# Every expert pair behind the branches to the further rounds, three branches for seven trips, and an earlier start for four weight chunks

## The chip, the cores and the metric

The kernel runs on one core of a Trainium2 chip. The metric is the device time of one execution in microseconds, the median over several. The engines are TensorE (PE in the rows), VectorE (DVE), ScalarE (ACT), GpSimd (POOL) and SyncE (SP), which issues nearly all DMAs.

## What is computed

One decoder block on 512 tokens of width 1024. The first half mixes tokens: a norm, a wide input projection, retention and an mLSTM, gates, an output projection and a residual add. Nothing of its arithmetic changes. The second half is a mixture of 32 experts, of which each token uses two:

```python
group_prob = softmax(xf @ w_group + b_group); g_w, g_idx = top_k(group_prob, 1)
top_logits, e_idx = top_k(sel_logits, TOP_K)          # 2 of the 8 experts of that group
weights = g_w * softmax(top_logits)
def expert_block(args):                               # 1024 -> 512 -> 1024 per expert
    xb, e = args
    return (silu(xb @ w_gate[e]) * (xb @ w_up[e])) @ w_down[e]
out = segment_sum(ys * slot_w[:, None], slot_tok, ...)  # residual add and final norm follow
```

All 32 experts are passed whatever the routing says, so 192 MB-sized pieces of weights are always read.

## The kernel before

Each engine has a program written by hand; the order on it is the order of the code, and engines wait for each other by semaphores. Of the mixture:

- **Pairs.** Two experts are worked on at once, each with up to 64 tokens (`CAP`): 16 pairs, one `pair` each. A pair's weights are 12 chunks of 1 MiB (`moe_chunk`): four of gate, four of up, four of down. They go through a ring of 18 slots, `raw_moe`, of 8 KB per partition. A slot's chunk is loaded when TensorE has used what was in it (`wait_chunk_used`), and no more than four chunks are in flight (`IN_FLIGHT`).
- **TensorE in a pair.** `gate_or_up` four times (half a gate or up product, 16 matmul rows in the trace, two chunks used), `turn_x` (transposes the next pair's gathered tokens), `turn_h`, `down` twice, and `combine` of the pair before (adds its result to the tokens). `last_pair` is the 16th pair.
- **The tables.** The router's result becomes two tables: which token sits in which slot (`tok_tab`; the product in line 723 makes it, and GpSimd gathers rows of x by it into `xg`), and which weight (`slot_tab`; product of line 733).
- **Rounds.** An expert with more than 64 tokens needs more rounds. Each engine reads the largest count with `value_load` and passes a loop of seven trips (`Fori(1, ROUNDS, 1)`), with an `If(most > r * CAP)` over the code of a whole round in it. With these inputs no round runs, and every trip jumps over the body. In front of this loop stand 15 pairs, behind it the 16th: the loop stands at line 774 on TensorE and at line 411 on SyncE, where the last 12 chunks are issued behind it.
- **The opening.** Into the ring go first 8 chunks, as the places of older tiles come free (lines 391 to 397), then `x2` is stored to `x_scratch` for the gather (line 400), then 8 chunks more, and the last two after the router's logits (`lg_ps`), since their slots lie on `h2T`.

Of the kernel before, what the change touches and what calls it, by code (L numbers as in the profile page):

```python
# [68 lines left out]
LAST_CHUNKS = R_CHUNKS - PAIR_CHUNKS  # L69
SP_LOOPS = (LAST_CHUNKS - MOE_RAW) // (2 * MOE_RAW)  # L70
# [23 lines left out]
def hybrid_block(nc, x, norm_mix_w, w_in, ret_gn_w, w_ret, conv_w, conv_b, b_i, b_f, mlstm_gn_w, w_mlstm, w_out,  # L94
                 norm_ffn_w, w_group, b_group, w_router, b_router, w_gate, w_up, w_down, norm_final_w, consts, out):
    ctx = ExitStack()
    with ctx:
# [6 lines left out]
        def sem(name):  # L104
# [27 lines left out]
                   enumerate([64, 72, 0, 8, 16, 24, 80, 88, 32, 40, 48, 56, 96, 104, 112, 120, 144.5, 152.5])]  # L132
# [9 lines left out]
        h2T = at("h2T", 144.5, [P, KD, T])  # L142
# [12 lines left out]
        squares = at("squares", 168.5, [P, TT, D])  # L155
# [19 lines left out]
        def small(name, shape, dt=F32):  # L175
# [64 lines left out]
        at_ok = sem("slots_ready")  # L240
# [21 lines left out]
            "one_hot_ready", "table_in_psum", "table_ready", "counts_ready"))  # L262
# [17 lines left out]
        def wait_chunk_used(eng, r, i, m):  # L280

            n, kind, half, a = chunk_of(m)
            if half == 0:
                eng.wait_ge(first_used, r * (6 * PAIRS) + i * (6 * LOOP_PAIRS) + 6 * n + 2 * kind + 2)
            else:
                eng.wait_ge((g_f, u_f, y_f[1])[kind], r * (2 * PAIRS) + i * (2 * LOOP_PAIRS) + 2 * n + 2)

# [15 lines left out]
        def _(sp):  # L303
# [72 lines left out]
            def round_chunks(r):  # L376
                if not isinstance(r, int):
                    for m in range(LAST_CHUNKS, R_CHUNKS):
                        moe_chunk(m, r - 1, 0, True)
                    for m in range(MOE_RAW):  # L380
                        moe_chunk(m, r, 0, True)
# [3 lines left out]
                for m in range(MOE_RAW + SP_LOOPS * 2 * MOE_RAW, LAST_CHUNKS):  # L385
                    moe_chunk(m, r, 0, True)
# [28 lines left out]
            for m in range(LAST_CHUNKS, R_CHUNKS):  # L415
                moe_chunk(m, extra, 0, True)
# [9 lines left out]
        def _(pe):  # L426
# [211 lines left out]
            def gate_or_up(r, i, n, up, half):  # L638
# [4 lines left out]
                if half == 0 and (not isinstance(N, int) or N > 0):  # L643
# [19 lines left out]
            def down(r, i, n, half):  # L663

                N, m = r * PAIRS + i * LOOP_PAIRS + n, PAIR_CHUNKS * n + 8 + 2 * half
                if half == 0:
                    pe.wait_ge(hf_ok, N + 1)
                    if not isinstance(N, int) or N > 0:
# [45 lines left out]
            def moe_round(r):  # L714
                N0 = r * PAIRS
                if not isinstance(r, int):
                    last_pair(r - 1)
                    combine(N0 - 1, range(8))
# [8 lines left out]

                pe.wait_ge(at_ok, r + 1)
                pe.wait_ge(ww_ok, 1)
                for n in range(2 * TT):  # L730
# [6 lines left out]
                turn_x(N0, 0)  # L737
                turn_x(N0, 1)
                for half in range(2):
                    gate_or_up(r, 0, 0, 0, half)  # L740
                for half in range(2):
                    gate_or_up(r, 0, 0, 1, half)
                turn_x(N0 + 1, 0)
                turn_h(N0)
                down(r, 0, 0, 0)
                turn_x(N0 + 1, 1)
                down(r, 0, 0, 1)
# [45 lines left out]
        def _(act):  # L793
# [191 lines left out]
            def square(t):  # L985
                act.wait_ge(free[t], BLOCKS)
                nc.scalar.activation(squares[:, t, :], x2[:, t, :], ACT.Square, accum_out=ssq[:, t:t + 1]).then_inc(sq_ok, 1)
# [19 lines left out]
            act.wait_ge(e2_ok, 1)  # L1007
            nc.scalar.activation(stat[:, 1, 0:TT], rt[:, 6, 0:TT], ACT.Sigmoid)
# [16 lines left out]
            def moe_round(r):  # L1025
                N0 = r * PAIRS
                if not isinstance(r, int):
                    pair(N0 - 1, last=True)
                pair(N0, first=isinstance(r, int))
                with act.Fori(0, PAIRS - 2, 1) as i:  # L1030
                    pair(N0 + i + 1)

            moe_round(0)
            act.wait_ge(cnt_ok, 1)
            most = act.value_load(cnt[0:1, 0:1], min_val=0, max_val=T)
            with act.Fori(1, ROUNDS, 1) as r:
                with act.If(most > r * CAP):
                    moe_round(r)


            extra = act.value_load(cnt[0:1, 1:2], min_val=0, max_val=ROUNDS - 1)
            pair(extra * PAIRS + (PAIRS - 1), last=True)
# [13 lines left out]
        def _(dve):  # L1056
# [354 lines left out]
            def pair(N, first=False, last=False, bare=False):  # L1411
# [16 lines left out]
                if first:  # L1428
                    dve.wait_ge(ir_in, 16)
# [6 lines left out]
            def moe_round(r):  # L1436
                N0 = r * PAIRS
                if not isinstance(r, int):

                    pair(N0 - 1, last=True)  # L1440
                    add(N0 - 1, range(8))
# [8 lines left out]
                V.tensor_tensor(at_slot[:, :, :, :].rearrange("p k t s -> p (k t) s"), where, slots, ALU.is_equal).then_inc(at_ok, 1)  # L1450
                if isinstance(r, int):
                    own(V.reduce_max(rt[:, 7, 40:41], cb[:, 1, TT * NE:(TT + 1) * NE], AX.X))
                dve.wait_ge(tab_ps, r * 2 + 2)
                V.tensor_scalar(tok_tab[:, :], cb[:, 2, 0:PAIRS], float(NO_TOKEN), None, ALU.add).then_inc(tab_ok, 1)
                if isinstance(r, int):
                    weights()
# [187 lines left out]
```

## Time and profile before

| | us |
|---|---|
| median of 3 runs (lowest, highest) | 1087.26 (1085.89, 1087.49) |
| the profiled execution, its own time | 1088.14 |
| span of its trace | 1086.4 |
| TensorE busy | 1013.1 |
| the mixture's pairs, from the first gate matmul to the last pair's down | 599 to 1069 |

The time of the profiled execution is 1.7 us over its span, and 0.9 us over the median. "Issue" in a chain is time in which an engine waited for nothing that the profile shows. A q behind an engine's name means its sequencer: PEldq is that of TensorE.

### The profile page before, as it was taken

The page shows a single profiled execution, that of the slowest core. Times are in us where ns is not written, and L with a number is a line of the kernel's source. Part 1 is how long each engine was busy: PE and PEld are TensorE (multiplying, and loading weights), DVE is VectorE, ACT ScalarE, POOL GpSimd, SP SyncE. Part 2 cuts the span into 40 slices and gives each one's busy share as a digit, 9 for nine tenths or more (in the row PEclk, how much of TensorE's full clock was granted, in tenths as well). Part 3 has the DMA queues.
Part 4 walks back from the last instruction along what each step waited for, and adds up shares of the span by engine and source line. Part 5 has one row for each costly group of instructions (what it writes and reads, how often), then busy time and mean ns, then how long its engine had stood idle before and what let it go on. Part 6 is the DMA issues. An engine that isn't in the chain of part 4 may idle for free.

```text
span 1086.4 us, 12967 instructions
## 1 busy us (share of the span) xinstructions
PE 1013.1 (93%) x4661; PEld 649.7 (60%) x4661; DVE 425.0 (39%) x733; ACT 276.6 (25%) x462; POOL 70.4 (6%) x102
## 2 busy tenths in 40 slices
PE   4999999999999999999993999999999999889874
PEld 4888888888888888888883333333333333333322
DVE  4236356434533334535524123333333232333316
ACT  5343564433333336413221000000000000000002
POOL 0564000000000000000000000000000000000000
PEclk9999999999999999999995999999999999999978
DMA  7313222222222222245829799999999999999791
GB/s 273 116 55 141 78 78 78 78 78 78 78 78 78 93 101 79 77 127 171 328 109 395 303 421 420 420 421 421 421 421 420 420 417 421 421 420 418 303 383 78
DMA packets 59959, 263.83 MB, mean 243 GB/s; under 512 B 9152, under 2 KB 9216, under 8 KB 35208
## 3 DMA queue, kind: packets, MB, share of 16 engines
q1 hardware_dynamic: 57432, 257.94, 60.2%
q0 software_dynamic: 2480, 5.26, 1.3%
q8 instruction: 30, 0.49, 0.2%
q14 instruction: 17, 0.14, 0.0%
HBM read 263.17 MB, written 4.20 MB: 246 GB/s over the span
## 4 chain that ended last, share of the span: by engine, by line
PE 55%; DMA 39%; issue 2%; DVE 2%; SPq 1%; ACT 0%; DVEq 0%; POOLq 0%; ACTq 0%
PE pj L463 45%; DMA raw_moe<-in_w_gate_dram 13%; DMA raw_moe<-in_w_up_dram 13%; DMA raw_moe<-in_w_down_dram 12%; PE pj L650 2%; PE cb L429 2%; DMA xg<-x_scratch,tok_tab 1%; PE cb L608 1%; PE cb L482 1%; PE pj L676 1%; PE cb L508 1%; DMA vrow<-in_mlstm_conv_w_dram 1%; PE cb L550 1%; PE cb L512 0%; PE cb L515 0%
## 5 line engine op out<-in xcount | busy, mean ns | idle before, releaser
L650 PE MATMUL pj<-raw_moe,xT 128*64 128x512 f32 x1024 | 233.0, 604 | 25.2 <-issue 10.2
L1070 DVE TENSOR_TENSOR wl<-raw_mix,wh 128x1024 fp32r<-128x1024 f32 x88 | 109.1, 1245 | 183.3 <-ACT wh L807 183.0
L650 PEld LDWEIGHTS pj<-raw_moe,xT 128*64 128x64 f32 x1024 | 75.1, 139 | 168.0 <-issue 168.0
L463 PE MATMUL pj<-wh,hTh 128*128 128x512 f32 x320 | 130.1, 407 | 1.6 <-DVE hTl L1098 1.6
L463 PE MATMUL pj<-wl,hTh 128*128 128x512 f32 x320 | 125.3, 392 | 0.0
L463 PE MATMUL pj<-wh,hTl 128*128 128x512 f32 x320 | 125.0, 391 | 0.0
L807 ACT ACTIVATE wh<-raw_mix 128x1024 fp32r<-128x1024 f32 x88 | 92.4, 1057 | 121.9 <-PE pj L463 111.1
L1403 DVE TENSOR_TENSOR x<-x,cb 128x512 f32<-128x512 f32 x120 | 77.0, 683 | 103.7 <-PE cb L687 103.7
L676 PE MATMUL pj<-raw_moe,hf 128*64 128x512 f32 x512 | 116.7, 598 | 0.8 <-ACT hf L1018 0.8
L463 PE MATMUL pj<-hTh,wh 128*128 128x512 f32 x192 | 80.2, 418 | 0.0
L463 PE MATMUL pj<-hTh,wl 128*128 128x512 f32 x192 | 75.4, 393 | 0.0
L463 PE MATMUL pj<-hTl,wh 128*128 128x512 f32 x192 | 75.1, 391 | 0.0
L676 PEld LDWEIGHTS pj<-raw_moe,hf 128*64 128x64 f32 x512 | 34.2, 136 | 67.0 <-issue 66.8
L463 PEld LDWEIGHTS pj<-wh,hTh 128*128 128x128 f32 x320 | 60.2, 188 | 13.7 <-issue 2.1
L463 PEld LDWEIGHTS pj<-wl,hTh 128*128 128x128 f32 x320 | 60.1, 188 | 13.0
L463 PEld LDWEIGHTS pj<-wh,hTl 128*128 128x128 f32 x320 | 60.3, 188 | 11.8
L1023 ACT ACTIVATE yh<-pj,now 128x512 fp32r<-128x512 f32 x32 | 20.4, 684 | 159.6 <-PE cb L687 143.6
L686 PE MATMUL cb<-yh,hot 128*128 128x512 f32 x124 | 55.0, 444 | 1.3 <-DVE yl L1433 0.8
L1414 DVE SCALAR_TENSOR_TENSOR sg<-pj,now,sg 128x512 f32<-128x512 f32 x16 | 12.0, 751 | 110.0 <-ACT sg L1014 110.0
L687 PE MATMUL cb<-yl,hot 128*128 128x512 f32 x124 | 49.2, 397 | 0.0
L1018 ACT ACTIVATE hf<-cb 128x512 f32<-128x512 f32 x16 | 9.6, 597 | 151.7 <-PE cb L429 151.7
L1408 DVE TENSOR_TENSOR xT<-cb,nwc 128x512 f32<-128x512 f32 x32 | 22.0, 689 | 60.6 <-PE cb L429 60.6
(274 smaller groups left out, 1217.4 us busy)
## 6 DMA issues: line engine op xcount, KB each, us to landing
raw_moe<-in_w_gate_dram SPq DMA_DIRECT2D x64, 1024.0 KB, 9.7
raw_moe<-in_w_up_dram SPq DMA_DIRECT2D x64, 1024.0 KB, 10.1
raw_moe<-in_w_down_dram SPq DMA_DIRECT2D x64, 1024.0 KB, 9.7
raw_mix<-in_w_in_dram SPq DMA_DIRECT2D x32, 1024.0 KB, 5.0
raw_mix<-in_w_ret_branch_dram SPq DMA_DIRECT2D x4, 1024.0 KB, 5.1
raw_mix<-in_w_mlstm_branch_dram SPq DMA_DIRECT2D x4, 1024.0 KB, 5.6
raw_mix<-in_w_out_dram SPq DMA_DIRECT2D x4, 1024.0 KB, 5.2
xt<-in_x_dram SPq DMA_DIRECT2D x4, 512.0 KB, 5.2
```

Source lines behind the costliest of these rows:

```text
L429: return nc.tensor.transpose(o, i, kc[0:k, K_IDENT:K_IDENT + k])
L463: m = nc.tensor.matmul(pj[:, i, :], lhsT, rhs, start=k == 0 and n == 0, stop=k == KD - 1 and n == 2)
L650: mm = nc.tensor.matmul(pj[a * CAP:(a + 1) * CAP, up, :], xT[:, 4 * half + k, a * CAP:(a + 1) * CAP], raw_moe[(m + a) % MOE_RAW][:, k, :], ...
L676: mm = nc.tensor.matmul(pj[a * CAP:(a + 1) * CAP, 2 + c, :], hf[:, 2 * half + f, a * CAP:(a + 1) * CAP], raw_moe[(m + a) % MOE_RAW][:, 2 * ...
L686: nc.tensor.matmul(bank, hot[:, t * P:(t + 1) * P], yh[:, c * 512:(c + 1) * 512], start=True, stop=False)
L687: return nc.tensor.matmul(bank, hot[:, t * P:(t + 1) * P], yl[:, c * 512:(c + 1) * 512], start=False, stop=True)
L807: nc.scalar.activation(wh[:, q % RING, :, :], raw_mix[n % MIX_RAW][:, 2 * (q % 2):2 * (q % 2) + 2, :], ACT.Copy).then_inc(wh_ok, 1)
L1023: nc.scalar.activation(yh[:, c * 512:(c + 1) * 512], pj[:, 2 + c, :], ACT.Copy, scale=now[:, 1:2]).then_inc(yh_ok, 1)
L1070: V.tensor_tensor(wl[:, q % RING, :, :], raw_mix[n % MIX_RAW][:, 2 * (q % 2):2 * (q % 2) + 2, :], wh[:, q % RING, :, :].bitcast(F32), ALU. ...
L1403: V.tensor_tensor(part, part, cb[:, 2 + g % 2, :], ALU.add).then_inc(c_add, 1)
L1408: V.tensor_tensor(xT[:, ks, :], cb[:, part, :].rearrange("p (k n) -> p k n", k=4), nwc[:, ks].unsqueeze(2).to_broadcast([P, 4, P]), ALU.mu ...
L1414: V.scalar_tensor_tensor(sg[:, :], pj[:, 0, :], now[:, 2:3], sg[:, :], ALU.mult, ALU.mult).then_inc(q_ok, 1)
```

## The change

- **The rounds' branches.** `further_rounds` takes the place of the loop: three branches, one for round 1, one for rounds 2 and 3, one for rounds 4 to 7, each over a body of its own with the code of a whole round in it (the second and third with a loop inside). On all engines but SyncE they stand ahead of the 16 pairs: on TensorE behind the first pair's gate product, on VectorE and ScalarE ahead of the first pair, on GpSimd behind the first gather. All 16 pairs follow as `all_pairs(extra)`. On SyncE they stand behind all 192 chunks.
- **The opening gate.** TensorE makes the token table, then the first gate; the weight table comes after the branches. The count of rounds (`extra`) has a semaphore of its own, `rounds_ok`, and VectorE makes the largest count ahead of the token table, the weights behind it.
- **The ring.** `h2T` moves away and the squares get two small tiles, so that the slots come in another order: chunks 8 and 9 are issued when the last weight tail of the mixing half is made (`wl_ok`), 10 and 11 after its 86th weight piece is used, all four ahead of the store of `x2`; 12 to 17 follow the store, and none waits for the logits.

```diff
-LAST_CHUNKS = R_CHUNKS - PAIR_CHUNKS
-SP_LOOPS = (LAST_CHUNKS - MOE_RAW) // (2 * MOE_RAW)
+SP_LOOPS = (R_CHUNKS - MOE_RAW) // (2 * MOE_RAW)
...
-                   enumerate([64, 72, 0, 8, 16, 24, 80, 88, 32, 40, 48, 56, 96, 104, 112, 120, 144.5, 152.5])]
+                   enumerate([64, 72, 0, 8, 16, 24, 80, 88, 144.5, 152.5, 96, 112, 32, 40, 48, 56, 104, 120])]
...
-        h2T = at("h2T", 144.5, [P, KD, T])
+        h2T = at("h2T", 168.5, [P, KD, T])
...
+        def further_rounds(eng, most, one_round):
+
+            for lo, hi in ((1, 2), (2, 4), (4, ROUNDS)):
+                with eng.If(most > lo * CAP):
+                    if hi - lo == 1:
+                        one_round(lo)
+                    else:
+                        with eng.Fori(lo, hi, 1) as r:
+                            one_round(r)
...
+            sp.wait_ge(wl_ok, MIX_PAIRS)
+            moe_chunk(8, 0, 0, False)
+            moe_chunk(9, 0, 0, False)
+            wait_mix_pair(sp, MIX_PAIRS - 3)
+            moe_chunk(10, 0, 0, False)
+            moe_chunk(11, 0, 0, False)
             for t in range(TT):
                 sp.wait_ge(free[t], BLOCKS)
                 sp.dma_start(x_dram[t * P:(t + 1) * P, :], x2[:, t, :]).then_inc(st_in, 16)
-            for m in range(8, 16):
+            for m in range(12, MOE_RAW):
                 moe_chunk(m, 0, 0, False)
...
-            sp.wait_ge(lg_ps, 1)
-            for m in range(16, MOE_RAW):
-                moe_chunk(m, 0, 0, False)
             round_chunks(0)
             sp.wait_ge(cnt_ok, 1)
             most = sp.value_load(cnt[0:1, 0:1], min_val=0, max_val=T)
-            with sp.Fori(1, ROUNDS, 1) as r:
-                with sp.If(most > r * CAP):
-                    round_chunks(r)
-            extra = sp.value_load(cnt[0:1, 1:2], min_val=0, max_val=ROUNDS - 1)
-            for m in range(LAST_CHUNKS, R_CHUNKS):
-                moe_chunk(m, extra, 0, True)
+            further_rounds(sp, most, round_chunks)
...
-            moe_round(0)
+            def one_round(r):
+                all_pairs(r - 1)
+                combine(r * PAIRS - 1, range(8))
+                token_table(r)
+                first_gate(r)
+
+            token_table(0)
+            first_gate(0)
             pe.wait_ge(cnt_ok, 1)
             most = pe.value_load(cnt[0:1, 0:1], min_val=0, max_val=T)
-            with pe.Fori(1, ROUNDS, 1) as r:
-                with pe.If(most > r * CAP):
-                    moe_round(r)
-
+            further_rounds(pe, most, one_round)
+            pe.wait_ge(rounds_ok, 1)
             extra = pe.value_load(cnt[0:1, 1:2], min_val=0, max_val=ROUNDS - 1)
-            last_pair(extra)
+            all_pairs(extra)
```

What this makes of TensorE's program at the opening. Rows 2315 to 2318 of it before (`cb<-what,at` is the token table's product, `cb<-wrhot,at_slot` the weight table's, `pj<-raw_moe,xT` a gate or up product):

```order
L723 MATMUL cb<-what,at_139 64x16 x16
L733 MATMUL cb<-wrhot,at_slot 64x32 x16
L429 MATMUL cb<-kc,xg 128x128 x8
L650 MATMUL pj<-raw_moe_72,xT 64x512
```

TensorE's program now at the same place, the gate's last matmul and what follows it:

```order
L727 MATMUL cb<-what,at_140 64x16 x16
L437 MATMUL cb<-kc,xg 128x128 x8
L658 MATMUL pj<-raw_moe_72,xT 64x512
...
L658 MATMUL pj<-raw_moe_75,xT 64x512
L793 TENSOR_LOAD cnt
L793 ISA x2
L293 COMPARE_AND_BRANCH
```

And behind the third branch's body, 1,660 rows further down, where the pairs go on with the weight table and the first up product:

```order
L297 COMPARE_AND_BRANCH
L293 UNCONDITIONAL_BRANCH
L796 TENSOR_LOAD cnt
L796 ISA x2
L733 REGISTER_ALU
L739 MATMUL cb<-wrhot,at_slot 64x32 x16
L311 ISA
L658 MATMUL pj<-raw_moe_76,xT 64x512
```

The first branch is at row 2335; behind the bodies it jumps over lie rows 2848 (the second branch), 3422 (the third) and 3996. The weight table moved from ahead of the first gate to behind all three. Before, the loop and the jump stood behind the 15th pair's last `combine`, and from there the body of 570 rows was jumped over:

```order
L686 MATMUL cb<-yh,hot 128x512
L687 MATMUL cb<-yl,hot 128x512
L773 TENSOR_LOAD cnt
L773 ISA x2
L774 UNCONDITIONAL_BRANCH
L774 ISA
L775 COMPARE_AND_BRANCH
```

SyncE's queue before, where it comes to the last down chunks of the 15th pair:

```order
L368 DMA raw_moe_88<-in_w_down_dram 128x2048
L368 DMA raw_moe_89<-in_w_down_dram 128x2048
L410 TENSOR_LOAD cnt
L410 ISA x2
L411 UNCONDITIONAL_BRANCH
L411 ISA
L412 COMPARE_AND_BRANCH
```

And now, where it comes to those of the 16th:

```order
L380 DMA raw_moe_82<-in_w_down_dram 128x2048
L380 DMA raw_moe_83<-in_w_down_dram 128x2048
L423 TENSOR_LOAD cnt
L423 ISA x2
L293 COMPARE_AND_BRANCH
```

The branch moved behind the last chunk; behind it only the four stores of the output are left.

## Rows read from the trace of the kernel before

**Rows 1.** The page: the span, and the chain that ended last by engine

```profile
span 1086.4 us, 12967 instructions
...
PE 55%; DMA 39%; issue 2%; DVE 2%; SPq 1%; ACT 0%; DVEq 0%; POOLq 0%; ACTq 0%
```

**Rows 2.** Chain in order of time (start, us, what): middle and end of the pairs

```profile
654.03 9.79 DMA raw_moe<-in_w_gate_dram
...
991.88 11.06 DMA raw_moe<-in_w_gate_dram
1003.09 9.79 DMA raw_moe<-in_w_up_dram
...
1014.46 5.26 issue
...
1025.02 0.35 SPq L373
```

**Rows 3.** Windows: core 0, us, busy of each engine, granted clock, DMA share, GB/s

```profile
548.00:560.00 12.00, 12.00 (x55) 9.94 (x54) 0.00 (x0) 0.00 (x0) 0.00 (x0) 1.00 0.01 1
577.00:586.00 9.00, 0.64 (x15) 0.45 (x14) 7.77 (x33) 1.91 (x4) 0.95 (x1) 0.50 1.00 421
592.00:597.00 5.00, 0.00 (x0) 0.00 (x0) 0.00 (x0) 0.00 (x0) 0.00 (x0) 0.50 0.83 342
600.00:602.00 2.00, 2.00 (x10) 0.69 (x8) 0.00 (x0) 0.00 (x0) 1.07 (x2) 0.66 0.18 29
604.00:606.00 2.00, 2.00 (x12) 0.78 (x10) 0.00 (x0) 0.00 (x0) 0.00 (x0) 1.00 0.33 66
606.00:608.00 2.00, 2.00 (x12) 0.68 (x10) 0.00 (x0) 0.62 (x1) 0.00 (x0) 1.00 0.99 418
1020.00:1026.00 6.00, 6.00 (x30) 2.50 (x28) 1.89 (x4) 0.00 (x0) 0.00 (x0) 1.00 0.04 16
1039.20:1045.00 5.80, 5.73 (x14) 1.92 (x16) 0.00 (x0) 0.00 (x0) 0.00 (x0) 0.50 1.02 424
```

**Rows 4.** Chain in order of time, opening of the pairs

```profile
588.28 8.65 DMA xg<-x_scratch,tok_tab
...
597.07 1.95 PE cb L429 x8
599.04 4.82 PE pj L650 x16
...
604.12 0.36 SPq L373
```

**Rows 5.** DMA of 598 to 604: issues, engine, op, count, us to landing

```profile
xg<-x_scratch,tok_tab POOLq DMA_INDIRECT x1, 3.3
```

**Rows 6.** Timeline of TensorE: start, us, line, operation, count, idle before

```profile
589.22 1.93 PE L733 MATMUL cb<-wrhot,at_slot 128*64 128x32 f32 x32 [2.27 <-DVE wrhot L1391]
...
599.04 15.08 PE L650 MATMUL pj<-raw_moe,xT 128*64 128x512 f32 x64
...
1039.27 13.39 PE L650 MATMUL pj<-raw_moe,xT 128*64 128x512 f32 x48 [10.19 <-issue]
...
1053.72 3.65 PE L650 MATMUL pj<-raw_moe,xT 128*64 128x512 f32 x16
```

**Rows 7.** Branches by line: count, ns least/median/most, first and last start

```profile
L775 PEldq COMPARE_BRANCH  x7: 221/221/6627, 1026.6 to 1037.6; - x7
...
L778 PEldq TENSOR_LOAD <-cnt x1: 322/322/322, 1038.1 to 1038.1; - x1
...
L1474 DVEq COMPARE_BRANCH  x7: 63/63/69, 1031.7 to 1036.2; - x7
```

**Rows 8.** DMA of 690 to 984 by queue: packets, MB, share

```profile
q1 hardware_dynamic: 16606, 120.95, 99.0%
q0 software_dynamic: 1440, 2.61, 2.4%
```

**Rows 9.** DMA of 1026.6 to 1033.3 by queue, TensorE's first jump

```profile
q8 instruction: 1, 0.02, 0.9%
```

More of the change, by code:

```diff
@@ L376, in round_chunks @@
             def round_chunks(r):
-                if not isinstance(r, int):
-                    for m in range(LAST_CHUNKS, R_CHUNKS):
-                        moe_chunk(m, r - 1, 0, True)
+                if not is_first(r):
                     for m in range(MOE_RAW):
@@ L384, in round_chunks @@
                         moe_chunk(m, r, i, True)
-                for m in range(MOE_RAW + SP_LOOPS * 2 * MOE_RAW, LAST_CHUNKS):
+                for m in range(MOE_RAW + SP_LOOPS * 2 * MOE_RAW, R_CHUNKS):
                     moe_chunk(m, r, 0, True)
@@ L636, in turn_x, with gate_or_up @@
                 m.then_inc(xT_ps, 1)
-            def gate_or_up(r, i, n, up, half):
+            def gate_or_up(r, i, n, up, half, first=False):
                 N, m = r * PAIRS + i * LOOP_PAIRS + n, PAIR_CHUNKS * n + 4 * up + 2 * half
@@ L642, in gate_or_up @@
                     pe.wait_ge(xT_ok, N * 2 + (half + 1))
-                if half == 0 and (not isinstance(N, int) or N > 0):
+                if half == 0 and not first:
                     pe.wait_ge((q_ok, h_ok)[up], N)
@@ L661, in turn_h, with down @@
                 m.then_inc(ht_ps, 1)
-            def down(r, i, n, half):
+            def down(r, i, n, half, first=False):
                 N, m = r * PAIRS + i * LOOP_PAIRS + n, PAIR_CHUNKS * n + 8 + 2 * half
@@ L667, in down @@
                     pe.wait_ge(hf_ok, N + 1)
-                    if not isinstance(N, int) or N > 0:
+                    if not first:
                         pe.wait_ge(yl_ok, N * 2)
@@ L712, in last_pair, with token_table @@
                 down(r, 0, n, 1)
[L714 to L718, printed above, removed]
+            def token_table(r):
                 pe.wait_ge(hot_ok, r + 1)
@@ L1023, in pair, with all_pairs @@
                     nc.scalar.activation(yh[:, c * 512:(c + 1) * 512], pj[:, 2 + c, :], ACT.Copy, scale=now[:, 1:2]).then_inc(yh_ok, 1)
-            def moe_round(r):
+            def all_pairs(r):
                 N0 = r * PAIRS
-                if not isinstance(r, int):
-                    pair(N0 - 1, last=True)
-                pair(N0, first=isinstance(r, int))
+                pair(N0, first=True)
                 with act.Fori(0, PAIRS - 2, 1) as i:
                     pair(N0 + i + 1)
-            moe_round(0)
+                pair(N0 + (PAIRS - 1), last=True)
             act.wait_ge(cnt_ok, 1)
             most = act.value_load(cnt[0:1, 0:1], min_val=0, max_val=T)
-            with act.Fori(1, ROUNDS, 1) as r:
-                with act.If(most > r * CAP):
-                    moe_round(r)
+            further_rounds(act, most, lambda r: all_pairs(r - 1))
+            nc.scalar.activation(stat[:, 1, 0:TT], onesq[:, 0:TT], ACT.Sigmoid)
+            act.wait_ge(rounds_ok, 1)
             extra = act.value_load(cnt[0:1, 1:2], min_val=0, max_val=ROUNDS - 1)
-            pair(extra * PAIRS + (PAIRS - 1), last=True)
+            all_pairs(extra)
             def final_square(t):
@@ L1409, in x_copy, with pair @@
                                 ALU.mult).then_inc(xT_ok, 1)
-            def pair(N, first=False, last=False, bare=False):
+            def pair(N, last=False, bare=False):
                 dve.wait_ge(now_ok, N + 1)
@@ L1434, in pair, with tables @@
                                            ALU.mult, ALU.subtract).then_inc(yl_ok, 1)
-            def moe_round(r):
+            def tables(r):
                 N0 = r * PAIRS
-                if not isinstance(r, int):
-                    pair(N0 - 1, last=True)
-                    add(N0 - 1, range(8))
+                if not is_first(r):
                     dve.wait_ge(it_ok, r)
@@ L1465, in moe_round, with one_round @@
-                x_copy(N0, 1)
-                pair(N0, first=isinstance(r, int), bare=True)
+                pair(N0, bare=True)
                 with dve.Fori(0, PAIRS - 2, 1) as i:
                     pair(N0 + i + 1)
-            moe_round(0)
+                pair(N0 + (PAIRS - 1), last=True)
+            def one_round(r):
+                all_pairs(r - 1)
+                add(r * PAIRS - 1, range(8))
+                tables(r)
+            tables(0)
+            dve.wait_ge(ir_in, 16)
             most = dve.value_load(cnt[0:1, 0:1], min_val=0, max_val=T)
-            with dve.Fori(1, ROUNDS, 1) as r:
-                with dve.If(most > r * CAP):
-                    moe_round(r)
+            further_rounds(dve, most, one_round)
@@ L1478, in _ @@
             extra = dve.value_load(cnt[0:1, 1:2], min_val=0, max_val=ROUNDS - 1)
-            pair(extra * PAIRS + (PAIRS - 1), last=True)
+            all_pairs(extra)
             dve.wait_ge(wf_in, 16)
@@ L1545, in _, with gather @@
             pool.wait_ge(zero_ok, 4)
-            def gather(N, n, copies=0):
-                if not isinstance(N, int) or N > 0:
+            def gather(N, n, copies=0, first=False):
+                if not first:
                     pool.wait_ge(xT_ps, N * 2)
@@ L1560, in gather, with columns @@
                                         bounds_check=T - 1, oob_is_err=False).then_inc(gat, 16)
-            def columns(N, n):
-                if not isinstance(N, int) or N > 0:
+            def columns(N, n, first=False):
+                if not first:
                     pool.wait_ge(yl_ok, N * 2)
@@ L1615, in constants @@
     k[:, K_PRIO:K_PRIO + NE] = NE - np.arange(NE)
-    k[:, K_LIMIT:K_LIMIT + ROUNDS - 1] = CAP * np.arange(1, ROUNDS)
+    for r in range(1, ROUNDS):
+        k[:, K_LIMIT + r - 1] = CAP * 2 ** (r.bit_length() - 1)
     k[:, K_ROW:K_ROW + T] = np.arange(T)
```

78 lines of the change are left out of this document (45 added, 33 removed).

## Prediction

> **What bounds the kernel.** I read the page first, then the chain in order of time, the windows by stretch, and the branches line by line. From about 600 us on the pairs wait for weights: the chain runs from one chunk's landing to the next, and TensorE is fast enough to wait. DMA is 39% of the chain that ended last, against 55% for TensorE, most of that from the mixing half [rows 1]. The reader should see the pace in two rows: the gate chunks that the chain passes at 654.03 and at 991.88 are 11 pairs apart [rows 2], so a pair takes 337.85 / 11 = 30.7 us, a chunk 2.56 us. A change can then only gain where this stream of chunks stands still, and there are two such places.
>
> At the end: SyncE takes the branch of the loop and resumes 5.3 us later; the six further trips take until it issues the next gate chunk at 1025.02 [rows 2]. The stream has run dry: 16 GB/s in 1020 to 1026 [rows 3]. TensorE takes its own branch, 6.6 us the first time [rows 7], and begins the last pair only at 1039.27, at half its clock (0.50) until 1045 [rows 3, 6]. It is so late that the last pair waits for it and not for its chunks.
>
> At the opening: the ring of 18 is full and the stream stands again, from about 592 + 5 x 342/421 = 596.1 to 605.7 (a window of 66 GB/s, then 418) [rows 3]. It waits for the first half gate, which waits for the gather: 8.65 us from issue to landing beside chunks at 421 GB/s, where the next gather, in a quiet stretch, took 3.3 us [rows 3 to 5].
>
> **The end, gain.** The last 12 chunks now follow without a branch. The up chunk of the 15th pair that the chain passes lands at 1003.09 + 9.79 = 1012.9 [rows 2]; the same chunk of the 16th then lands at 1043.6, and the last half up product starts there, not at 1053.72 [rows 6]. What stands behind it (down, combine, the last norm, the stores: 1086.4 - 1053.7 = 32.7 us) is kept, and its down chunks, 6 us behind at the pace of before, are in time as in every pair. Gain: 10.0 us. SyncE's own three branches now lie behind its last issue. At 5.3 us each they take 16 us from about 1050 (the last chunk's issue), to 1066; the first output can be stored only when the last norm is done, behind the last down product, which ends 17 us before the end. They cost nothing, with at least 3 us of cover.
>
> **The opening, gain.** In 548 to 560 the DMAs moved 1 GB/s [rows 3]. Four chunks go there, 4 x 2.5 = 10 us of the busy stretch behind it, so the ring is full at about 586 and the first gather, issued at 588.28, finds quiet queues: 3.3 us for 8.65. The weight table's 1.93 us [rows 6] was made while TensorE waited for the gather, so taking it from there gives nothing. Transposes, then gate: half 1 starts at 599.04 - 5.35 = 593.7 and ends, with the 4.8 us of the row, at 598.5; half 2 ends at 601.9 (64 rows in 15.08, less the slow part: 3.43 a half) [rows 4, 6]. The stream restarts 5.3 us sooner too, at 600.4. The slower clock of the first microseconds is as before: granted 0.66 in 600 to 602 [rows 3], 4.3 us behind the first transpose.
>
> **The opening, price: three jumps on TensorE.** This is what decides. The sequencer runs some 15 matmuls ahead (it took its branch at 1026.6, while half a down product was still to run), so it reads the count at 598.6 and stands at the first branch at 599.7. What does a jump cost? One row shows it from both sides: of seven trips six took 221 ns, and the first 6,627 ns [rows 7]; in that first one an instruction packet was fetched [rows 9], and the seventh's target is the first's. VectorE's jumps, over a short body, all took some 63 ns [rows 7]. Each of the three new branches has a target of its own, over 500 rows beyond the branch. So I count three first passes, none of the cheap kind.
>
> The Trainium skill ("Runtime: NRT & Kernel Launch", section on instruction fetch mechanics) says the same: a taken branch whose target isn't in the two-page window must fetch the page before execution goes on. It also says that the window is only two 16 KiB lines, and there the trace differs: the loop of three pairs ran from 690 to 984 with no instruction packet at all [rows 8], and six trips found both ends of a long body. So a target that was passed once stays cheap, and one that was not, does not.
>
> Both first passes (6.6 us on TensorE, 5.3 on SyncE) fell into stretches with chunks in flight. With quiet queues the fetch should be shorter, as the gather was: bounds are 6.6 and, if the fetch shrank like the gather (3.3 of 8.65), 2.5; I take 4.3, nearer the middle. The first jump (599.7) comes just ahead of the restarted stream: 4.3. The second falls into the four chunks that half a gate and its fellow released, 600.4 to 610.6: 6.7 with its branch. The third starts at 610.7, when those have landed: 4.3. Sum 15.3: out at 615.0. Reading the second count takes 1.1 us (1038.1 to the matmul at 1039.27) [rows 6, 7], the weight table 1.93, now in the open, and half an up product. TensorE has idled 14 us and is at half clock again. After 1039.2 that lasted 5.8 us and after the gather 4.3; I take 5 from 616.1: the half ends at 616.1 + 1.9 + 4.9 = 622.9.
>
> Only this half releases chunk 23 of the stream, so its data begin at 622.9 + 1.9 = 624.8 (603.8 to 605.7 before). Before, the stream came to it at 605.7 + 4 x 2.56 = 615.9. Price: 8.9 us. From there on the pace of the DMAs holds, since TensorE has a full ring and needs about 27 us a pair, an estimate: six halves of 3.43, and some 6 us for transposes and combine.
>
> **Elsewhere.** VectorE, ScalarE and GpSimd take three branches each while TensorE takes its own; they are next needed at about 618 (VectorE), so even misses of 5 us each (three from 595) stay hidden, with some 7 us to spare; without that cover they would cost 63 ns to 5 us apiece. The largest count ahead of the token table is one small operation on one value and stands where VectorE waited for that table's product; the table itself is not later. The two square tiles and the place of `h2T` change no wait that lasts. Registers in the waits of the 14th to 16th pair cost sequencer time, which runs ahead: nothing. The four early chunks take DMA time from nobody in 548 to 560.
>
> **Sum.** From the profiled span [rows 1]: 1086.4 - 10.0 + 8.9 = 1085.3 us of span. The profiled execution lay 0.9 over the median, so I compare differences: 1087.26 - 1.1 = **1086.2 us**. A kernel this steady can be told apart at about 0.2%, 2.2 us.
>
> **Rivals.**
> 1. **Every jump at its full price** (slower). If a quiet queue does not shorten the fetch, the jumps end at 599.7 + 20 = 619.8, 4.8 later than in my sum, and the time is 1091.0. It is slower from a sum of about 18.5 us for the three. For it: the only price seen on TensorE is 6.6, and a target near a page's end can need a second page. Against: both prices were seen with chunks in flight. Chance 0.23.
> 2. **Short jumps** (faster). If a quiet fetch is nearer 2.5 us and the second is not slowed much, the sum is 12.5 or less, and the time 1083.4 or below. For it: the gather's 3.3 against 8.65. Chance 0.25.
> 3. **One miss or none** (faster by far). If the targets were there already, the branches would cost 0.2 us each [rows 7] and perhaps one fetch: out by 606, half the up product done at 612, and chunk 23 follows 614, about 2 us ahead of before. Time 1087.3 - 10.0 - 1.9 = 1075.4. For it: six of seven trips. Against: these six went to a target just visited. Chance 0.12. The Trainium skill ("Advanced Engine Details and Errata", section on control flow timing) gives a compare-and-branch about 108 ns; by that figure alone this case would hold. The row of 221 ns is the nearest to it; that of 6,627 speaks against it here.
> 4. My forecast, a near tie of two known amounts: 0.40.
>
> **Range and chances.** Cases 1 to 3 give 1075.4, 1083.4 and 1091.0. A range of 1081.5 to 1091.5 leaves out case 3 and a tail. Faster by over 0.2%: cases 2 and 3, 0.37. Within: 0.40. Slower: 0.23. If the forecast's own case holds, 1084.5 to 1088.5.
>
> **What the trace after will show.** (a) No stretch without chunks between the 15th and 16th pair, and the last half up starting 32.7 us before the end. (b) Near nothing of the DMAs between 586 and 600, the gather landing 3.3 us after its issue, the gate near 593.7. (c) Three first-pass branches on TensorE of 4 to 7 us each, and a second quiet stretch of the DMAs from about 610 to 625. (d) Half clock for the first up product. The forecast is wrong if the three together take under 13 or over 18 us, or if TensorE, late by a pair's share, does not keep up with the stream afterwards.

## The result, and the profile after

| | before | changed kernel |
|---|---|---|
| median, us | 1087.49 (20 runs) | 1088.69 (20 runs) |
| lowest, us | 1084.2 | 1087.11 |
| ratio to before, 95% interval | | 1.0014 (1.0007 to 1.002) |
| profiled execution: its own time, span, us | 1088.14, 1086.4 | 1087.22, 1085.4 |

The change makes the kernel slower by 0.14%, some 1.2 to 1.5 us. That is inside the 0.2% that I called no change and inside the range, but it goes the other way from my 1.1 us of gain. One run of the changed kernel (1745.98 us) and one of e10's six (2641.37 us) were disturbed: the ratios leave them out, and without them the two medians are 1088.64 and 1082.49.

The two profiled executions say the opposite, 1.0 us in favour of the change. So I looked first at where they part. The page and the chain of the changed kernel (start, us, what) through the opening:

```profile
span 1085.4 us, 12869 instructions
...
PE 56%; DMA 38%; issue 2%; DVE 2%; SPq 1%; ACT 0%; DVEq 0%; POOLq 0%; ACTq 0%
```

```profile
586.39 4.57 DMA xg<-x_scratch,tok_tab
...
591.10 1.95 PE cb L437 x8
593.08 8.73 PE pj L658 x32
601.80 13.75 issue
615.55 1.92 PE cb L739 x32
617.47 8.41 PE pj L658 x32
```

The new item is 13.75 us of "issue" between the gate and the weight table, where there was none before. TensorE's timeline, with the router's logits ahead of it and the last pair behind:

```profile
569.80 5.45 PE L616 MATMUL cb<-wrt,h2T 128*128 128x36 f32 x48
...
584.54 0.60 PE L727 MATMUL cb<-what,at 128*64 128x16 f16 x16 [1.94 <-DVE at L1459]
...
615.55 1.92 PE L739 MATMUL cb<-wrhot,at_slot 128*64 128x32 f32 x32 [13.75 <-issue]
617.25 8.59 PE L658 MATMUL pj<-raw_moe,xT 128*64 128x512 f32 x32
...
1048.07 3.65 PE L658 MATMUL pj<-raw_moe,xT 128*64 128x512 f32 x16 [1.36 <-DMA raw_moe<-in_w_up_dram]
...
1052.86 3.65 PE L658 MATMUL pj<-raw_moe,xT 128*64 128x512 f32 x16
```

At the end the last pair waits 1.36 us for a chunk, and the 10.19 us of issue [rows 6] are gone. The row to compare with is the token table at 584.54. Nothing of the change lies ahead of it that could speed it up, yet in the trace of before it starts at 586.34. The reader finds the 1.8 us in the logits: the 48 rows took 5.45 us here. In the trace of before the rows of that product reached 408 ns; in this one none is over 279:

```profile
L616 PE MATMUL cb<-wrt,h2T x64: 198/279/279, 567.1 to 575.0; 128*128 128x36 f32 x64
```

The same kernel profiled again (e1 below) has a row of 409 ns and its table at 586.71. So this is a difference between executions and not between kernels. From here on I count each trace **from the start of the token table to the end of the span**: before 1086.4 - 586.34 = 500.1 us, the changed kernel 500.9. Now trace and median agree in sign.

The branches by line (count, ns least/median/most, first and last start):

```profile
L293 ACTq COMPARE_BRANCH  x3: 45/45/45, 585.5 to 586.2; - x3
L293 POOLq COMPARE_BRANCH  x3: 45/45/50, 587.0 to 587.3; - x3
L293 DVEq COMPARE_BRANCH  x3: 56/56/72, 594.0 to 594.8; - x3
L293 PEldq COMPARE_BRANCH  x3: 3581/4972/7682, 598.2 to 609.6; - x3
L293 SPq COMPARE_BRANCH  x3: 45/50/53, 1054.1 to 1062.3; - x3
```

TensorE's three take 3.6 + 7.7 + 5.0 = 16.2 us. On the other engines each row is under 0.1 us, but on SyncE the row does not hold the jump's price: the second of its branches starts 5.2 us behind the first and the third 2.9 us behind the second, just as 5.26 us of "issue" stood behind its branch before [rows 2]. VectorE, too, issues nothing for 2.1 us behind its third row. On ScalarE and GpSimd the gaps are 0.1 to 0.4 us. Windows (PE, PEld, DVE, ACT, POOL busy; granted clock; DMA share; GB/s):

```profile
602.00:604.00 2.00, 0.00 (x0) 0.00 (x0) 0.00 (x0) 0.00 (x0) 0.00 (x0) 1.00 1.02 426
604.00:610.00 6.00, 0.00 (x0) 0.00 (x0) 0.00 (x0) 0.00 (x0) 0.00 (x0) 0.72 1.01 404
610.00:612.00 2.00, 0.00 (x0) 0.00 (x0) 0.00 (x0) 0.00 (x0) 0.00 (x0) 0.50 0.29 86
612.00:616.00 4.00, 0.45 (x9) 0.48 (x10) 0.00 (x0) 0.00 (x0) 0.00 (x0) 0.50 0.06 23
616.00:624.00 8.00, 8.00 (x54) 3.62 (x54) 0.95 (x2) 0.69 (x1) 0.18 (x1) 0.73 0.11 16
...
634.00:636.00 2.00, 2.00 (x13) 0.60 (x10) 0.75 (x1) 0.69 (x1) 0.89 (x1) 1.00 0.91 229
636.00:638.00 2.00, 2.00 (x12) 0.70 (x10) 0.75 (x1) 0.69 (x1) 0.03 (x1) 1.00 0.94 352
...
1036.00:1056.00 20.00, 18.33 (x82) 6.62 (x78) 5.04 (x8) 3.44 (x5) 0.18 (x1) 1.00 1.01 420
```

From 602 to 615.5 TensorE does nothing while its clock falls to 0.50. The chunks that the gate freed are loaded by 610, and then the stream stands until 624. At the end it runs through at 420 GB/s. So one stall has gone and another has come.

### The profile page after: what moved, and what is told of

Its sections match the earlier page's. It is cut to its first block, busy times and chain, and to the rows that moved or that the text cites. A ratio compares the mean times of both kernels' runs of the same rounds, so it can differ in the third digit from the quotient of the medians.

```text
span 1085.4 us, 12869 instructions
## 1 busy us (share of the span) xinstructions
PE 1010.1 (93%) x4661; PEld 646.4 (60%) x4661; DVE 424.7 (39%) x733; ACT 276.6 (25%) x462; POOL 70.7 (7%) x102
## 3 DMA queue, kind: packets, MB, share of 16 engines
q0 software_dynamic: 2480, 5.26, 1.3%
## 4 chain that ended last, share of the span: by engine, by line
PE 56%; DMA 38%; issue 2%; DVE 2%; SPq 1%; ACT 0%; DVEq 0%; POOLq 0%; ACTq 0%
PE pj L471 45%; DMA raw_moe<-in_w_up_dram 13%; DMA raw_moe<-in_w_down_dram 12%; DMA raw_moe<-in_w_gate_dram 12%; PE pj L658 2%; PE cb L437 2%; PE pj L684 1%; PE cb L490 1%; DMA vrow<-in_mlstm_conv_w_dram 1%; PE cb L616 1%; PE cb L516 1%; PE cb L558 1%; PE cb L523 0%; PE cb L520 0%; PE cb L497 0%
## 5 line engine op out<-in xcount | busy, mean ns | idle before, releaser
L658 PE MATMUL pj<-raw_moe,xT 128*64 128x512 f32 x1024 | 232.5, 602 | 15.3 <-DMA raw_moe<-in_w_up_dram 7.8
```

Of the source, the lines that this page charges most:

```text
L658: mm = nc.tensor.matmul(pj[a * CAP:(a + 1) * CAP, up, :], xT[:, 4 * half + k, a * CAP:(a + 1) * CAP], raw_moe[(m + a) % MOE_RAW][:, k, :], ...
```

## The experiments

Theory A: the three first jumps of TensorE set the restart of the chunk stream, and their sum decides the sign. Its rival, theory B: the steady part is slower (16 pairs whose waits go against registers), or the new gate order or the branch instructions themselves cost the time. All counts "to the end" are from the token table's start to the end of the span.

| kernel | to the end, us | median, us (before) | ratio, 95% interval |
|---|---|---|---|
| before | 500.1 | | |
| changed | 500.9 | 1088.69 (1087.49) | 1.0014 (1.0007 to 1.002) |
| e1, changed again | 501.5 | 1089.39 (1087.19) | 1.002 (1.0009 to 1.0031) |
| e2, no branches on TensorE | 485.5 | 1073.84 (1087.19) | 0.9886 (0.9871 to 0.9901) |
| e3, one guard | 487.8 | 1075.3 (1087.19) | 0.9894 (0.9878 to 0.991) |
| e4, branches first | 493.9 | 1082.83 (1087.19) | 0.9964 (0.995 to 0.9978) |
| e5, one guard, first | 484.4 | 1073.29 (1087.14) | 0.9866 (0.9851 to 0.9881) |
| e6, four branches | 506.7 | 1093.74 (1087.14) | 1.0057 (1.0043 to 1.0071) |
| e7, quiet branches | 501.4 | 1089.95 (1087.14) | 1.0025 (1.0015 to 1.0034) |
| e8, new ring only | 494.45 | 1082.88 (1087.14) | 0.9963 (0.995 to 0.9977) |
| e9, short bodies | 485.1 | 1073.16 (1087.25) | 0.9875 (0.9854 to 0.9895) |
| e10, two branches | 494.2 | 1082.53 (1087.25) | 0.9955 (0.9939 to 0.997) |
| e11, old ring | 505.0 | 1092.52 (1087.25) | 1.0044 (1.0032 to 1.0055) |
| e12, SyncE's tail only | 499.1 | 1086.92 (1087.25) | 0.9995 (0.9985 to 1.0005) |

Many of the forecasts below missed by a little. Counted to the end, e5 came 1.6 us under its range, e10 1.3, e9 0.9, e8 0.5 and e12 0.4, and the ratios of e2, e3 and e4 lie 0.001 to 0.003 above theirs. None of these misses changes which theory an experiment speaks for.

**e1, the changed kernel again.** No edit; to see how far two executions of it lie apart.

> The changed kernel once more, unchanged, for a second trace. Theory A (the three jumps behind the opening gate give back what the end gained): each first pass over a far target costs TensorE 3.5 to 8 us, 16 us in all as in the first trace, and the time is within 0.3% of before; jumps that differ by a few us from execution to execution explain why the first trace ended 1.0 us earlier than that of before and the median came 1.2 us later. Theory B (the jumps are not what counts; waits with registers and the pairs as one dynamic piece slow the steady pace): the pair period is above the 30.7 us of before by 0.1 us or more.

```profile
570.02 7.41 PE L616 MATMUL cb<-wrt,h2T 128*128 128x36 f32 x48
...
586.71 0.60 PE L727 MATMUL cb<-what,at 128*64 128x16 f16 x16 [1.94 <-DVE at L1459]
...
618.17 1.92 PE L739 MATMUL cb<-wrhot,at_slot 128*64 128x32 f32 x32 [14.93 <-issue]
```

```profile
L293 PEldq COMPARE_BRANCH  x3: 3756/5112/8503, 599.7 to 612.1; - x3
```

Three jumps of 17.4 us here, with a stall of 14.93 us: the sum moves by over 1 us between executions of one kernel. The slow logits are the usual case: of the 14 traces of this document 11 have a row of 407 to 409 ns there, and three (the changed kernel's first, e2 and e9) have none over 279. By theory B a pair should have become longer by 0.1 us. The gate chunks that the chain passes, ten pairs apart, lie 307.3 us apart before (684.61 to 991.88), 307.6 in the changed kernel (689.40 to 997.04) and 307.8 in e1 (692.04 to 999.82): 30.73, 30.76 and 30.78 us a pair. The pace is the same to 0.05 us.

**e2, no branches on TensorE.** What it lacks: a routing that needs a second round would not be served.

```diff
             most = pe.value_load(cnt[0:1, 0:1], min_val=0, max_val=T)
-            further_rounds(pe, most, one_round)
             pe.wait_ge(rounds_ok, 1)
```

> TensorE takes no branch at all (the branches to further rounds are left out on TensorE alone, so a routing that needs a second round would not be served; with these inputs the same work is done). Theory A: TensorE goes from gate to up with only 1 us between, the stream of chunks never stands after 600 us, span 1071 to 1073, ratio to before 0.986. Theory B: the time stays above 1080.

```profile
584.53 0.60 PE L727 MATMUL cb<-what,at 128*64 128x16 f16 x16 [1.94 <-DVE at L1458]
...
593.10 8.72 PE L658 MATMUL pj<-raw_moe,xT 128*64 128x512 f32 x32
601.64 1.08 PE L739 MATMUL cb<-wrhot,at_slot 128*64 128x32 f32 x32
602.54 7.08 PE L658 MATMUL pj<-raw_moe,xT 128*64 128x512 f32 x32
```

```profile
612.00:1035.00 423.00, 404.54 (x1816) 159.36 (x1818) 137.13 (x215) 39.24 (x61) 19.55 (x43) 1.00 1.01 420
```

All registers in waits and the whole new gate order are still there, and the end comes 15.4 to 16.0 us sooner. The weight table costs 1.08 us at full clock, against 1.92 behind the stall, and the stream holds 420 GB/s for 423 us. Theory B's registers and gate order fall.

**e9, short bodies.** The same three branches on TensorE, taken, but over one instruction each. This too serves no second round.

```diff
-            further_rounds(pe, most, one_round)
+            further_rounds(pe, most, lambda r: pe.sem_inc(pe_past, 1))
```

> The changed kernel with TensorE's three branches at their place, but over bodies of one semaphore instruction in place of a whole round (TensorE alone; a routing that needs a second round would not be served). Tells the branch from the distance. If the far target is the price: 0.2 to 0.4 us a branch, 486 to 487 us from token table to end, ratio 0.987 to 0.990, near the kernel without jumps (485.5). If a branch in itself stops TensorE, 5 us each and 500.

```profile
L293 PEldq COMPARE_BRANCH  x3: 202/207/230, 598.2 to 598.7; - x3
```

0.2 us each, without any instruction packet on TensorE's queue (q8) between 598.1 and 605, and 485.1 to the end, as without any branch. The rest of theory B falls: the price is of the far target, not of the branch. The Trainium skill ("Advanced Engine Details and Errata", section on control flow timing) gives a compare-and-branch about 108 ns; TensorE's take twice that here, the other engines' half of it.

**e10 and e6, two and four branches.** The first has branches over `((1, 2), (2, ROUNDS))`, the second this:

```diff
-            for lo, hi in ((1, 2), (2, 4), (4, ROUNDS)):
+            for lo, hi in ((1, 2), (2, 3), (3, 4), (4, ROUNDS)):
...
-        k[:, K_LIMIT + r - 1] = CAP * 2 ** (r.bit_length() - 1)
+        k[:, K_LIMIT + r - 1] = CAP * min(r, 4)
```

> Two branches (round 1; rounds 2 to 7) behind the opening gate. With 485.5, 487.8, 501.2 and 506.7 us from token table to end for none, one, three and four: jumps of about 3.7 and 8 us put TensorE's weight table at 611.5 to 613, the third quiet jump's 5 us are saved: 495.5 to 497 us, ratio 0.996 to 0.998.

> Four branches instead of three behind the opening gate (rounds 2 and 3 each by its own). Theory A: one more first pass in a quiet stretch, 4.7 to 5.3 us, all of it visible: 506 to 507 us from token table to end, ratio 1.006 to 1.008. If only the first passes near chunks in flight counted, it would stay at 501.

TensorE's branches of e10, then of e6:

```profile
L293 PEldq COMPARE_BRANCH  x2: 3422/5530/7638, 599.6 to 603.0; - x2
```

```profile
L293 PEldq COMPARE_BRANCH  x4: 3661/4950/8702, 600.0 to 617.3; - x4
```

With none, one (e3), two, three and four branches the end lies 485.5, 487.8, 494.2, 500.9 to 501.5 and 506.7 us behind the table. The first costs only 2.3 us, since most of it passes while TensorE still has matmuls queued. The further ones cost 6.4, 6.7 to 7.3 and 5.2 to 5.8 us to the end, against rows of 7.6, 5.0 to 5.1 and 5.1 us. So each costs about its whole length. The third costs 1.7 to 2.2 us more than that; up to 0.9 us of it is the second row, which is longer there than in e10, and the rest has no row of its own.

**e3, one guard in the same place.** The three branches stand inside one, so that a kernel without further rounds passes one.

```diff
-            for lo, hi in ((1, 2), (2, 4), (4, ROUNDS)):
-                with eng.If(most > lo * CAP):
-                    if hi - lo == 1:
-                        one_round(lo)
-                    else:
+            with eng.If(most > CAP):
+                one_round(1)
+                for lo, hi in ((2, 4), (4, ROUNDS)):
+                    with eng.If(most > lo * CAP):
                         with eng.Fori(lo, hi, 1) as r:
```

> One outer branch (largest count above 64) holds all three, on all engines: TensorE jumps once, at the same place. Theory A: one jump of about 3.6 us, ring deep enough to hide it, span 1071 to 1074, ratio 0.986 to 0.988. A variant of A in which a longer jump costs more (the target is 1,660 rows away and not 513): the one jump takes well over 4 us, and some of it shows. Theory B: above 1080.

```profile
L292 PEldq COMPARE_BRANCH  x1: 3536/3536/3536, 600.6 to 600.6; - x1
```

TensorE sat idle 0.96 us in place of 13.75. The jump now goes as far as all three did before, and costs no more than the first of them: the length of one jump does not grow with the distance, here at least.

**e4, the three branches ahead of the first gate**, where TensorE waits for the gather anyway.

```diff
                 N0 = r * PAIRS
+                first_gate(r)
                 slot_table(r)
...
                 token_table(r)
-                first_gate(r)
 
             token_table(0)
-            first_gate(0)
```

> The three branches stand ahead of TensorE's first gate, where it waits for the gather, and not behind it. Theory A: jumps from about 586, 3.6 to 5 us each, out at 598 to 601, so the gate starts some 8 us later than in the changed kernel, but nothing stops the stream after it: span 1079 to 1081, ratio 0.994. Theory B: no change against the changed kernel, 1085.

```profile
L293 PEldq COMPARE_BRANCH  x3: 3376/4724/5103, 588.2 to 596.8; - x3
```

Sum 13.2 us, with no chunk in flight, and some 6 us of it under the wait for the gather. The gate starts 9.0 us later behind the table than in the changed kernel, and the end still comes 7 us sooner.

**e5, one guard, ahead of the first gate** (the edits of e3 and e4 together).

> One outer branch around the three, and ahead of TensorE's first gate. From token table to end: before 500.1 us, changed kernel 500.9 and 501.5. Theory A: the one jump of 3.4 to 4 us lies behind the gather, which lands 6 us after TensorE's token table; with the read of the count TensorE is at its transposes when the rows land or at most 1 us later; nothing stops the stream: 486 to 487 us from token table to end, ratio 0.987 to 0.989, at or a little under that of the kernel with one guard behind the gate (487.8 in its trace). Rival C (a quiet queue makes no difference, the jump takes over 5 us and delays the gate by 2): 489.

```profile
L292 PEldq COMPARE_BRANCH  x1: 3434/3434/3434, 587.8 to 587.8; - x1
```

```profile
592.91 1.96 PE L436 MATMUL cb<-kc,xg 128*128 128x128 f32 x8 [5.68 <-DMA xg<-x_scratch,tok_tab]
595.08 7.91 PE L657 MATMUL pj<-raw_moe,xT 128*64 128x512 f32 x32 [0.21 <-issue]
602.80 1.09 PE L738 MATMUL cb<-wrhot,at_slot 128*64 128x32 f32 x32
```

The jump ends at 591.2 and the gather's rows are used at 592.91: it is wholly hidden. With 0.9866 of before this is the best of the versions that keep every branch a full routing needs (e3, the next, has 0.9894, and the two intervals just touch). In no run here was a further round taken.

**e7, quiet branches.** SyncE holds every chunk behind the ring's first filling until TensorE has made the weight table.

```diff
+            sp.wait_ge(wt_ps, 2)
             round_chunks(0)
```

> The changed kernel, but SyncE holds chunk 19 and all behind it until TensorE's weight table is made, so that all three jumps meet quiet DMA queues. If chunks in flight are what makes the second jump long (7.7 and 8.5 us), it takes 4.5 to 5.3 here, the three together 13 to 14 us instead of 16.2 to 17.4; if it is something else about the second target, it stays near 8. The end comes 0 to 3 us later than in the changed kernel, since four chunks move behind the jumps.

```profile
L293 PEldq COMPARE_BRANCH  x3: 3704/4664/4731, 600.5 to 609.0; - x3
```

Without chunks in flight the longest jump falls from 7.7 or 8.5 us to 4.7; the three take 13.1. The gain goes into the chunks that are held back meanwhile. So the load of the DMAs makes some 3 to 4 us of the second jump; the first is 3.4 to 3.8 us in every kernel.

The rest of a jump's length is in the instruction packets, 16 KB each, that TensorE's queue (q8) fetches during it. The changed kernel's first, second and third jump (598.2 to 601.9, to 609.6, to 614.7):

```profile
q8 instruction: 1, 0.02, 1.6%
q8 instruction: 2, 0.03, 3.1%
q8 instruction: 2, 0.03, 4.5%
```

With the start of a jump's first packet, from the same traces, each jump splits in two (us):

| jump | row | packets | from its start to the first packet | from there to its end |
|---|---|---|---|---|
| changed, first | 3.58 | 1 | 1.23 | 2.35 |
| changed, second | 7.68 | 2 | 3.62 | 4.06 |
| changed, third | 4.97 | 2 | 0.90 | 4.07 |
| e7, first | 3.70 | 1 | 1.03 | 2.67 |
| e7, second | 4.66 | 2 | 0.67 | 4.00 |
| e7, third | 4.73 | 2 | 0.69 | 4.04 |
| before, the only long one | 6.63 | 1 | 4.27 | 2.35 |

So two things set the price. The wait for the first packet depends on the load, and what follows it depends on whether one packet is fetched or two. The 6.6 us of before were one packet beside chunks; the second jump of the changed kernel is two packets beside chunks.

**e8 and e11, the ring alone, and all but the ring.** e8 is the kernel before with the change's ring: the order of slots, the places of `h2T` and the squares, and SyncE's order at the opening. e11 is the changed kernel with the slots, `h2T` and SyncE's opening order of before.

> The kernel before with the changed ring alone (four chunks in the quiet stretch ahead of the store, h2T moved, squares in two tiles); loop and last pair as before. Theory A: the first gather lands in 4 to 5 us and not 8.7, the gate starts 4 to 5 us after the end of the token table's wait sooner, and all of it reaches the end, since nothing else stops the stream earlier: 495 to 496 us from token table to end, ratio 0.995 to 0.996. Rival: the end waits for TensorE's jump anyway and takes nothing of it (500).

> The changed kernel with the ring as before (chunks 9 to 12 behind the store of x2, the last two behind the logits). The gather lands in 8.7 us and not 4.5, so gate and jumps come about 4 us later: 505 to 506 us from token table to end, ratio 1.005 to 1.007. If the jumps were shorter in the other traffic, less.

TensorE in e8:

```profile
592.71 1.95 PE L432 MATMUL cb<-kc,xg 128*128 128x128 f32 x8 [1.37 <-DMA xg<-x_scratch,tok_tab]
594.69 14.46 PE L653 MATMUL pj<-raw_moe,xT 128*64 128x512 f32 x64
...
1034.23 13.11 PE L653 MATMUL pj<-raw_moe,xT 128*64 128x512 f32 x48 [10.16 <-issue]
```

The ring alone gives 5.6 us (500.1 to 494.45; by the medians 4.3); taking it from the changed kernel costs 3.5 to 4.1. It works through the gather, which took 4.1 us here, and 8.9 in e11, as before [rows 4].

**e12, SyncE's tail alone.** The kernel before, with all 192 chunks issued ahead of SyncE's loop; TensorE's loop stays.

```diff
-LAST_CHUNKS = R_CHUNKS - PAIR_CHUNKS
+LAST_CHUNKS = R_CHUNKS
...
-                    for m in range(LAST_CHUNKS, R_CHUNKS):
-                        moe_chunk(m, r - 1, 0, True)
...
-            for m in range(LAST_CHUNKS, R_CHUNKS):
-                moe_chunk(m, extra, 0, True)
```

> The kernel before, but SyncE issues all 192 chunks ahead of its loop of seven; TensorE's loop stays behind 15 pairs. If TensorE's own late start bounds the last pair, as the forecast says, nothing is gained: 499.5 to 500.5 us from token table to end, ratio 1.000 within 0.002. If SyncE's gap in the stream was the bound, up to 7 us come out.

```profile
1010.00:1036.00 26.00, 19.34 (x88) 8.23 (x84) 8.81 (x14) 1.86 (x3) 0.19 (x1) 0.93 1.01 417
```

```profile
1039.46 12.16 PE L646 MATMUL pj<-raw_moe,xT 128*64 128x512 f32 x48 [9.92 <-issue]
```

The gap in the stream is closed (417 GB/s in 1010 to 1036, where 1020 to 1026 had 16 [rows 3]), and the interval of the ratio still holds 1. Of the up to 7 us that SyncE's gap could have held, 1.0 at most comes out (500.1 to 499.1). TensorE's own late jump bound the end, not SyncE's.

## Why the prediction was wrong by its sign and near by its size

**The two amounts were the right ones.** The change takes a stall of ten microseconds from the end and puts one of nine or more into the opening. Measured from the token table, my sum says 1085.3 - 586.34 = 499.0 us; the two traces have 500.9 and 501.5. The error is 1.9 to 2.5 us, the difference forecast was 1.1, and so the sign turned.

**The end: right.** The stream has no gap, and from the start of the last half up it is 1085.4 - 1052.86 = 32.5 us to the end (forecast 32.7). SyncE's three branches start at 1054.1, 1059.4 and 1062.3 and the first output is stored at 1077.3: hidden, as said. They took 5.2 us, 2.9 us and an unknown time for the third, whose end no row shows. That TensorE's lateness was the bound there, e12 shows.

**The gather: the value taken was too low.** 4.57 us, not 3.3 (4.1 to 4.8 us in all kernels with the new ring). The gate starts 8.5 us behind the table, not 7.4. Little of it reached the branches: TensorE's sequencer met the first 13.7 us behind the table in one trace and 13.0 in the other, against 13.4 forecast, since it was further ahead of its matmuls than I took it to be.

**The three jumps: this is the step that failed, in size.** That they are three first passes, each with a price of its own, held; e2, e9 and the series of none to four show it. The sizes were to be 4.3, 6.7 and 4.3, sum 15.3. They were 3.6, 7.7 and 5.0 in one execution and 3.8, 8.5 and 5.1 in the other: 16.2 and 17.4. The first was cheaper than I took it, the second dearer than the only price seen, 6.6, and the third, in a quiet stretch, 5.0. I had scaled the quiet price from the gather's; e7 shows that the jumps shrink less than the gather does. And I had taken the one long jump on record, 6.6 us with one instruction packet [rows 9], as the full price of all three. The second and the third fetch two packets each: behind the start of the first packet they take 4.1 us where that one took 2.35. The other terms behind them, the count, the weight table and half an up product, came out 0.1 and 0.8 us longer together. SyncE can issue again 38.1 and 39.2 us behind the table (at 622.59 in the first trace), against 622.9 - 586.34 = 36.6. Of the whole error of 1.9 and 2.5 us the jumps, with the gaps between them, are 1.0 and 2.3. In the second trace they alone turn the sign. In the first they alone would have made a tie, and the later start (0.3) and the stretch behind the opening (0.6, below) did the rest.

**From there on: right, with one thing unforeseen.** From that issue to the last half up it is 430.3 us (1052.86 - 622.59) and 429.7 in e1; my sum has 1085.3 - 32.7 = 1052.6 for that half, and 1052.6 - 622.9 = 429.7. In 634 to 638 the stream falls to 229 and 352 GB/s. TensorE is in its transposes and down product from 625.9 on and frees nothing for 6 us, while only the few chunks freed on either side of that are in flight; that costs (2 x 192 + 2 x 69) / 421 = 1.2 us, of which at most 0.6 shows at the end. Where the rest is won back I did not find.

**The rivals.** Every jump at full price (slower, 0.23) would have made 19.9 us of the three (my 619.8 is 0.1 to 0.2 too high); 16.2 and 17.4 lie between it and my 15.3. Its reason, that a quiet queue does not shorten a jump, is false, but the second page that it counted in its favour is there in the second and the third. The sign turned well before its point of 18.5 us, which I had set for a loss of over 0.2%. Short jumps: no; even the quietest three (e7) took 13.1. One miss or none: no in this kernel, but the case itself exists and is what e9 measures, 485.1 to the end. The time forecast for it was 1075.4, the one measured 1073.16.

**The branches on the other engines** have rows of 45 to 72 ns, and what they cost stands behind the rows. VectorE's three start within 0.8 us, its next instruction comes 2.2 us behind the start of the third, at 596.98, and all of it lies ahead of its next work, as forecast.

**A trap.** The first profiled span, 1085.4, matches my 1085.3 nearly to the digit. It does so because that execution's logits ran faster, by 1.8 us, and my sum was too short by 1.9.

## What to carry to other kernels

An `If` over a large body that is not entered is no free test: it is a jump to code that isn't there, and on TensorE each first pass cost 3.4 to 8.7 us here, most when transfers are in flight, and 0.2 us over a short body. On SyncE a far jump cost 2.9 to 5.4 us, and only the gap behind the branch's row shows it. On ScalarE and GpSimd the same test, also over a whole round, cost at most 0.6 us. Put rare cases behind one guard with the others nested in it, and place the guard where the engine waits for something anyway: two such edits turned this slower change into a gain of 1.3% (e5, 0.9866 of before). And where two executions differ ahead of the edit, compare stretches from a common row behind that difference.

## What the runs showed of the hardware

- **A far jump's price is a wait and a fetch.** Over all the far jumps of TensorE in these traces, the first instruction packet starts 0.7 to 1.2 us behind the branch where no chunk is in flight or the last ones are just landing, and 3.5 to 4.7 us behind it where chunks run on. From there to the jump's end it is 2.3 to 2.7 us with one packet and 4.0 to 4.2 with two. The second jump took 7.6 to 8.7 us with chunks in flight (the changed kernel, e1, e6, e10, e11) and at most 5.1 in e4 and e7, without. The third of e11, into the end of its chunks, lies between: 6.5 us, with 2.4 to the first packet. The Trainium skill ("Runtime: NRT & Kernel Launch", section on instruction fetch mechanics) says that a taken branch to a target outside the window must fetch its page before execution goes on, and gives no price; the traces agree. The same second jump in the DMA queues, 601.9 to 609.6 of the changed kernel:

```profile
q1 hardware_dynamic: 424, 3.10, 97.4%
```

- **The first far jump of the opening fetches one packet**, in all eight kernels that have one there, and every further one fetches two. The first takes 3.4 to 3.8 us, and up to its packet the DMAs moved at most 8 GB/s. The only long jump of before, e8 and e12, with chunks in flight, fetches one packet too and takes 6.2 to 6.6 us. Why one needs one packet and another two was not settled; the distance is not it, since e3's single jump goes as far as all three and fetches one.
- **TensorE's clock can fall ahead of the logits' end or behind it.** In 574 to 575 the granted clock is 1.00 in the changed kernel's first trace and 0.50 in e1, the same program, with TensorE busy throughout in both. The longest row is then 279 or 409 ns, and all that follows moves by about 2 us. What decides between them was not tried.
